# Sixteen conditioning units moved from the feed-forward stage to the first attention

## The reference

```python
act_lat = silu(c)
act_ctx = silu(c_ctx)[None, :]
for layer in range(DEPTH):
    mod_lat = split((act_lat @ ada_w[layer] + ada_b[layer])[:, None, :], 6, axis=-1)
    mod_ctx = split((act_ctx @ ada_w[layer] + ada_b[layer])[:, None, :], 6, axis=-1)
    h_lat = modulate(x, g_pre_mix[layer], mod_lat[0], mod_lat[1])
    ...
    x = x + mod_lat[2] * rms_norm(y_lat, g_post_mix[layer])
```

## Time and profile before

| | us |
|---|---|
| median of 3 runs (1855.43 to 1861.6) | 1857.51 |
| the profiled execution | 1856.46 |
| its span, first to last instruction | 1854.7 |
| around the span | 1.76 |

### The profile page before, as it was taken

One profiled execution on the slowest core, in us unless ns is written; L12 is line 12 of the kernel. 1 busy time (PEld: TensorE's weight loads), 2 busy tenths in 40 slices (PEclk: granted clock), 3 DMA queues, 4 the chain that ended last, 5 costly groups with the idle time before them and its releaser, 6 DMA issues.

```text
span 1854.7 us, 21716 instructions
## 1 busy us (share of the span) xinstructions
PE 1708.6 (92%) x8938; PEld 1176.6 (63%) x8939; DVE 781.3 (42%) x942; ACT 663.0 (36%) x719; POOL 283.2 (15%) x104
## 2 busy tenths in 40 slices
PE   5998789999999988897899999999999999999995
PEld 2575467777777877646756566656656557666662
DVE  3257432222223346153754445644455535444343
ACT  4223433221122243443443433533434533333341
POOL 0100011100011021001312222212212211111110
PEclk8998799999999988898899999999999999999998
DMA  9770223544443123112599999999999999899990
GB/s 382 282 274 1 91 68 117 206 164 173 182 182 108 63 80 114 46 46 81 198 380 409 409 399 367 405 409 409 399 369 410 409 404 393 316 337 360 355 332 24
DMA packets 157910, 470.64 MB, mean 254 GB/s; under 512 B 8457, under 2 KB 34034, under 8 KB 151154
## 3 DMA queue, kind: packets, MB, share of 16 engines
q1 hardware_dynamic: 154610, 463.28, 66.2%
q10 hardware_dynamic: 3200, 5.96, 0.9%
HBM read 468.13 MB, written 1.07 MB: 253 GB/s over the span
## 4 chain that ended last, share of the span: by engine, by line
PE 73%; DMA 8%; DVE 7%; ACT 5%; POOL 3%; issue 2%; SPq 1%; DVEq 0%; ACTq 0%
PE PS L322 15%; PE PS L323 14%; PE PS L324 14%; PE PS L2216 7%; DMA raw<-in_moe_w_in_dram 4%; ACT high L294 3%; POOL low L303 3%; PE PS L2390 3%; PE PS L2231 3%; DVE low L303 2%; PE PS L1825 2%; DMA ah_behind<-in_moe_w_in_dram 2%; PE PS L2151 2%; PE PS L2152 2%; PE PS L2153 2%
## 5 line engine op out<-in xcount | busy, mean ns | idle before, releaser
L303 DVE TENSOR_TENSOR low<-raw,high 128x2048 fp32r<-128x2048 f32 (+3 forms) x171 | 353.0, 2072 | 388.5 <-ACT high L294 388.5
L294 ACT ACTIVATE high<-raw 128x2048 fp32r<-128x2048 f32 (+2 forms) x171 | 322.8, 1892 | 408.0 <-PE PS L324 242.8
L322 PE MATMUL PS<-high,ah 128*128 128x512 f32 (+2 forms) x918 | 368.0, 401 | 29.4 <-DVE low L303 11.9
L323 PE MATMUL PS<-low,ah 128*128 128x512 f32 (+2 forms) x918 | 358.0, 390 | 0.0
L324 PE MATMUL PS<-high,al 128*128 128x512 f32 (+2 forms) x918 | 357.1, 389 | 0.0
L303 POOL TENSOR_TENSOR low<-raw,high 128x1024 fp32r<-128x1024 f32 (+2 forms) x56 | 184.5, 3295 | 1111.9 <-ACT high L294 1097.2
L322 PEld LDWEIGHTS PS<-high,ah 128*128 128x128 f32 x918 | 174.1, 190 | 107.4 <-issue 32.4
L324 PEld LDWEIGHTS PS<-high,al 128*128 128x128 f32 x918 | 174.3, 190 | 36.0
L323 PEld LDWEIGHTS PS<-low,ah 128*128 128x128 f32 x918 | 174.5, 190 | 31.8
L322 PE MATMUL PS<-ah,high 128*128 128x512 f32 (+1 forms) x392 | 153.7, 392 | 2.5 <-issue 2.5
L323 PE MATMUL PS<-al,high 128*128 128x512 f32 (+1 forms) x392 | 151.1, 385 | 0.0
(11 more groups left out here) (360 smaller groups left out, 1792.3 us busy)
## 6 DMA issues: line engine op xcount, KB each, us to landing
raw<-in_moe_w_in_dram SPq DMA_DIRECT2D x150, 1024.0 KB, 14.0
raw<-in_moe_w_out_dram SPq DMA_DIRECT2D x75, 1024.0 KB, 11.0
raw<-in_ada_w_dram SPq DMA_DIRECT2D x48, 1024.0 KB, 7.5
X<-in_moe_w_in_dram SPq DMA_DIRECT2D x28, 1024.0 KB, 14.0
ah_behind<-in_moe_w_in_dram SPq DMA_DIRECT2D x25, 1024.0 KB, 13.7
raw<-in_ffn_w_in_dram SPq DMA_DIRECT2D x22, 1024.0 KB, 5.1
al_behind<-in_moe_w_in_dram SPq DMA_DIRECT2D x21, 1024.0 KB, 14.1
al_behind<-in_moe_w_out_dram SPq DMA_DIRECT2D x16, 1024.0 KB, 11.2
```

The source lines that it names most:

```text
L294: act.activation(high[n % SPL][:, 0:width], buf[:, 0:width], ACT.Copy).then_inc(high_made, 1)
L303: eng.tensor_tensor(low[n % SPL][:, c0:c1], buf[:, c0:c1], high[n % SPL][:, c0:c1].bitcast(F32), ALU.subtract).then_inc(low_made[n % SPL], 1)
L322: pe.matmul(o, sh, mh, start=start, stop=False)
L323: pe.matmul(o, sh, ml, start=False, stop=False)
```

## The change

Units 24 to 31 (group 3) run on PE ahead of the wait for `kn_ready`, into bank 6. Units 32 to 39 (group 4) run in steps 8 to 15 of the first attention, one a step, between the scores and the turn, into bank 7. Units 40 to 47 (group 5) stay in the feed-forward stage, one after each of steps 0 to 7. The ring's order and SP's loads follow. Group 3 is copied out in step 4 of the attention on DVE, turned in step 8 and taken in step 10; group 4 is copied out behind the attention and turned in the output projection, where the last row block (banks 6 and 7) of about 0 and 1 now comes behind the three others of both units. The two key heads are turned into banks 0 and 1, with a wait for `gate_rows`.

```diff
-ADA_AFTER = [2, 2, 2, 2] + [1] * 16 + [0, 0]
-ORDER = "a" * 8 + "m" + "a" * 4 + "m" + "aaaam" * 2 + "aaaa" + "m" * 8
+ADA_AFTER = [1] * 8 + [0] * 14
+ORDER = "a" * 8 + "m" + "a" * 4 + "m" + "aaaam" * 2 + "aaaa" + "m" * 4 + "a" * 8 + "aam" * 4
...
-ADA_DONE = [f for f in range(20) if sum(ADA_AFTER[:f + 1]) % 8 == 0]
+ADA_DONE = [7]
...
# att_pe, in step i behind scores(i):
+                if step:
+                    step(i)
...
# SyncE:
+            for a in range(24, 32):
+                load_ada(sp, a)
             for j in range(4):
+                load_ada(sp, 32 + 2 * j)
+                load_ada(sp, 33 + 2 * j)
                 load_unit(sp, N_ABOUT + j, about[:, 2 * j:2 * j + 2, :])
...
# VectorE:
+            def conditioning(i):
+                if i == 4:
+                    rows_copy(dve, 3, 6)
+                if i == 10:
+                    cols_take(dve, 3, 6)
+
+            att_dve(dve, 0, link, lambda j: vector_low(dve, N_ABOUT + j), conditioning)
+            rows_copy(dve, 4, 7)
+            cols_take(dve, 4, 6)
...
# TensorE:
+            pe.wait_ge(s["qk_ready"], 4)
+            for a in range(24, 32):
+                ada(a, 6)
             pe.wait_ge(s["kn_ready"], 1)
+            pe.wait_ge(s["gate_rows"], 1)
             for h in range(4, 6):
                 qk_turn(h)
             pe.wait_ge(s["qk_ready"], 6)
-            att_pe(pe, 0)
+
+            def conditioning(i):
+                if i == 8:
+                    ada_turn(3, 6)
+                if 8 <= i < 16:
+                    ada(24 + i, 7)
+
+            att_pe(pe, 0, conditioning)
...
             for j in range(2):
                 unit_ready(pe, N_ABOUT + j)
-                for b in range(NB):
-                    last = about_block(j, b)
-                last.then_inc(unit_used, 1)
+                for b in range(NB - 1):
+                    about_block(j, b)
+                if j == 0:
+                    pe.wait_ge(s["cols_taken"], 4)
+                    ada_turn(4, 6)
+            pe.wait_ge(s["cols_taken"], 5)
+            for j in range(2):
+                about_block(j, NB - 1).then_inc(unit_used, 1)
```

More of the change, by code:

```diff
@@ L616, in att_keys, with att_pe @@
             return (0, NTOK) if a == 1 or i < 8 else (SEQ, CTX)
-        def att_pe(pe, a):
+        def att_pe(pe, a, step=None):
             m = att[a]
@@ L708, in att_act, with att_dve @@
                     between(BETWEEN.index(i))
-        def att_dve(dve, a, link, between=None):
+        def att_dve(dve, a, link, between=None, step=None):
             m = att[a]
@@ L837, in _ @@
                     abin_unit(ch, kh)
+            for a in range(24, 32):
+                load_ada(sp, a)
             for j in range(4):
+                load_ada(sp, 32 + 2 * j)
+                load_ada(sp, 33 + 2 * j)
                 load_unit(sp, N_ABOUT + j, about[:, 2 * j:2 * j + 2, :])
-            a = 24
+            a = 40
             for j in range(11):
@@ L1020, in qk_move @@
                 act.wait_ge(s["qk_turned"], h + 1)
-                act.activation(qT[:, h, :] if h < 4 else kT[:, h - 4, :], PS[:, 6 + h % 2, :], ACT.Copy).then_inc(s["qk_ready"], 1)
+                act.activation(qT[:, h, :] if h < 4 else kT[:, h - 4, :], PS[:, 6 + h % 2 if h < 4 else h - 4, :], ACT.Copy).then_inc(s["qk_ready"], 1)
             for h in range(4):
@@ L1403, in _ @@
             cat_lower()
-            att_dve(dve, 0, link, lambda j: vector_low(dve, N_ABOUT + j))
+            def conditioning(i):
[6 more added lines that the diff above has]
+            cols_take(dve, 4, 6)
             vector_low(dve, N_ABOUT + 3)
@@ L1423, in _ @@
                 if f in ADA_DONE:
-                    rows_copy(dve, 3 + ADA_DONE.index(f), 4)
+                    rows_copy(dve, 5 + ADA_DONE.index(f), 4)
                 if f - 1 in ADA_DONE:
-                    cols_take(dve, 3 + ADA_DONE.index(f - 1), 7)
+                    cols_take(dve, 5 + ADA_DONE.index(f - 1), 7)
             def hidden_low(f):
@@ L1897, in qk_turn @@
                     t = Q[:, b, h * P:(h + 1) * P] if h < 4 else KV[:, b, (h - 4) * P:(h - 3) * P]
-                    last = pe.transpose(PS[:, 6 + h % 2, b * P:(b + 1) * P], t, ident)
+                    last = pe.transpose(PS[:, 6 + h % 2 if h < 4 else h - 4, b * P:(b + 1) * P], t, ident)
                 last.then_inc(s["qk_turned"], 1)
@@ L1971, in _ @@
                 if f - 1 in ADA_DONE:
-                    ada_turn(3 + ADA_DONE.index(f - 1), 7)
+                    ada_turn(5 + ADA_DONE.index(f - 1), 7)
             pe.wait_ge(s["cols_taken"], 6)
```

## The result

The changed kernel takes 1837.24 us (median of 4 runs, 1835.37 to 1838.13), the kernel before, run beside it, 1857.38: a ratio of 0.9896, 95% interval 0.9877 to 0.9915, so 20.1 us less. Measured a second time, the two took 1833.69 and 1856.12, ratio 0.9874 (0.9849 to 0.9900), 22.4 us less. Forecast were 15.5 us less.

The account below looks back on a forecast made before the run. PE was taken to bound the feed-forward stage, with the attention's path winding through PE, DVE and ACT. The terms sum to -15.5 us, from 1856.46 to 1841.0; with the median 1.05 above the profiled execution, forecast 1842.0 us, range 1835 to 1849.

Parts of the forecast that it names:

- Feed-forward, -18.6: Feed-forward stage: units and two of three turns leaving PE shorten it one for one, -18.6 us.
- Keys, +2.6: Ahead of the key turns: eight units, the last waiting for its load, delay the keys by 2.6 us.
- Clock at the attention's start, -1.4: Key turns and first scores: PE kept busy may hold the clock; half of 2.9 us taken, -1.4.
- DVE's copies, +0.9: Attention: group 3's copy in step 4 costs 0.7 us and its take in step 10 0.2.
- Step 8, +0.6: Attention step 8: turn and unit meet an idle gap of 0.69 us on PE, costing 0.6 us.
- The other seven units, 0: Attention up to step 15: 6.4 us of units fit into remaining waits of 11.2 us, cost 0, up to +3.
- Clock behind, 0 of a bound of -4: Attention's end and output projection's start: more PE work could hold the clock, up to -4 us; 0 taken.
- Output projection, +0.4: Output projection: one more turn costs 0.4 us; about 3 is ready just when PE wants it, 0, bound +0.5.
- Rival (a): PE keeps its clock through the attention: -21.0 us in all, 1836.5 us; chance 0.17.
- (b): Attention: the clock falls and the units don't fit; -10.1 us in all, 1847.4 us; chance 0.20.
- (c): Feed-forward stage gives nothing, PE only looked like the bound: +3.1 us, 1860.6 us; chance 0.09 with smaller losses.
- (d): Keys and attention: the ring's loads become PE stalls and the kernel gets slower, +8.7 us at 17 us a load; chance 0.04.

Follow-up runs that it names:

- The fillers: Kernel before plus seven products of a unit's shape, result unused, on PE ahead of the wait for the keys; 1854.12 us against 1855.06, ratio 0.9989.
- the half change: Against the kernel before: group 3 ahead of the keys, groups 4 and 5 one unit a step in feed-forward steps 0 to 15; 1843.81 us, ratio 0.9917.
- six units at the keys: Changed kernel with only units 24 to 29 ahead of the keys, the other ten in steps 8 to 16; 1830.93 us against 1833.69.

## Why the prediction came out as it did

- **Feed-forward, -18.6: right**, -19.08. The count was right. By whole steps of the kernel before, from first matmul to first matmul, a step takes 13.00 us with a pair and 12.11 with one unit, and 10.88 without any after the change: 2.12 and 1.23 us for what I had priced at 2.06 and 1.19. Summed over the 16 units these hundredths make the half us.
- **Keys, +2.6: right, with its cause.** +2.41 to +2.51; unit 31's load was the last to arrive, and with six units the delay is gone. Waits of 0.73 and 1.42 us stood where I had 0.3 and 1.7. The rule of the Trainium skill that the prediction cites ("DMA: Bandwidth & Descriptors", "Queues, rings and completion order") played no part: the second load released PE 2.5 us after the first.
- **Clock at the attention's start, -1.4: the mechanism right, the size off.** The full -2.5 came in all three profiles; I had halved the term for want of a row. The fillers show the term by itself; the half change shows that it isn't certain.
- **DVE's copies, +0.9: too much.** Step 4's copy takes 0.68 us and costs 0.49 (5.61 against 5.12 between values); with the copy in step 11 instead these are 5.12 again (six units at the keys). The take doesn't show.
- **Step 8, +0.6:** +0.46. **The other seven units, 0: the step that failed.** Units in steps 9 and 10 cost 1.0 us. I summed the gaps of the whole half and let ACT's and DVE's splits cover every step; between the values of steps 8 and 10 there were gaps of 0.61 and 0.19 us for two units of 0.92 each, which leaves the 1.0, and the wide gap beside the split comes only in step 11. With no unit in step 9 the cost is gone.
- **Clock behind, 0 of a bound of -4: the other miss.** From the values of step 16 to the projection -0.9 us in the first profile and -2.0 in the two others, and -1.7 to -1.9 in the projection, so -2.7 to -3.9 together. I argued from two gaps left in the last steps; at the projection the clock was up in spite of them in all three profiles. Over all profiles it was down there in the four without work in the steps (twice the kernel before, the fillers at the keys, the half change), and up in nine of the ten with some, even in the one with hardly any. So work in the steps went with the clock, but not each time, and what decides it stays open.
- **Output projection, +0.4:** the turn doesn't show (62.35 to 62.54 us with it, 62.39 and 62.43 without), and about 3 was no later than needed, as worked out.

The sum of the stages touched is +2.5 - 2.5 + 0.7 - 1.7 - 19.1 = -20.1 in the first profile (-21.5 in the second). The forecast of -15.5 was 4.6 short, and in part luck kept it that near: the 1.0 us of steps 9 and 10 that the sum left out hides as much of the clock's gain. Rival (a), at 1836.5 us, with a chance of 0.17, is nearest to what came, though its condition holds only in part, since the clock did fall once in the attention, and its -6.9 us for the clock were -5.2 to -6.4. How long the clock stays up was read too pessimistically from a kernel whose gaps were empty. Rivals (b) and (c) fell: the clock was kept at the keys and the units and the turn cost 1.5 us in steps 8 to 10, and the stage gave all. So did (d), since no load was awaited in steps 12 to 15; but the argument against it was weaker than it looked. The loads took 8.0 us in the median, not 4.8, and what saved the steps is the time between the use of unit 32 and that of unit 36, 11.8 us in the first profile (197.2 to 209.0).

## What to carry to other kernels

Work that leaves a stage where one engine never waits comes back one for one; what it costs at its new place has to be read step by step, gap by gap, not from a sum of gaps. When filling an engine's idle time, fill it with no more than is already loaded: here the seventh and eighth unit cost 2.5 us because their loads could only start when the first two were used. And price the clock on its own: useless work in the same gap shows what it is worth there, before anything is moved.

## What the runs showed of the hardware

The granted clock at one and the same instruction differs between executions of one kernel: 0.50 and 1.00 at the projection's start, 65.54 and 62.43 us for the stretch. The half change lost the clock over waits of 0.63 and 1.41 us with one unit between them; the changed kernel kept it over 0.73 and 1.42, and the six-unit form over a single one of 1.73. A conditioning load of 1 MB took 4.8 us in the median in the kernel before, with the DMA busy for 0.17 of the time from 170 to 225 us, and 8.0 in the changed kernel, with 0.77. The stretch ahead of the first query turn, where no kernel here changes what PE, ACT and DVE do, took between 157.8 and 164.3 us, so one profile's total says little about a change of 5 us, and its stages say much.
